# Loads of a feed-forward stage put in another order in a float32 decoder trunk on one TensorE

## The chip, the cores and the metric

The kernel runs on one core of a Trainium2 chip. The metric is the device time of one execution in microseconds (us); the kernel before takes 902.14 us, the median of three runs (898.80, 902.14 and 902.43). A profiled execution of its own took 899.16 us.

## The reference

The input x is 256 tokens by 1024 channels in float32. Two layers follow, each of three residual sub-layers: half a SwiGLU feed-forward, a token mixer, and half a second feed-forward. All weights are read once from HBM.

```python
for i in range(2):
    x = x + 0.5 * swiglu_ffn(rms_norm(x, ffn1_norm[i]), ffn1_w_in[i], ffn1_w_out[i])
    xn = rms_norm(x, mix_norm[i])
    y = pool_conv_mixer(xn, ...) if i % 2 == 0 else sgu_mixer(xn, ...)
    x = x + y
    x = x + 0.5 * swiglu_ffn(rms_norm(x, ffn2_norm[i]), ffn2_w_in[i], ffn2_w_out[i])
return rms_norm(x, final_norm)

def swiglu_ffn(x, w_in, w_out):              # w_in 1024 x 5632, w_out 2816 x 1024
    gate, up = jnp.split(x @ w_in, 2, axis=-1)
    return (jax.nn.silu(gate) * up) @ w_out
```

## The kernel before, in words

**Stages.** There are six, numbered k = 0 to 5: feed-forward (FFN), pooling and convolution mixer, FFN, FFN, gating mixer, FFN. So the four FFNs are stages 0, 2, 3 and 5; below they are the first to the fourth FFN.

**Slabs.** Weights arrive in slabs of 1 MB (128 partitions by 2048 floats, two DMAs of 512 KB each, issued by SP). Each slab is split into a high part (ScalarE, line 726, `w_hi`) and a low part (VectorE, line 1138, `w_lo`), since TensorE multiplies float32 as three products (lines 1676 to 1678). A slab of an FFN is named by its number in the stage, 0 to 38: slab 12 is `b + 12` in the code. Most slabs land in a ring of three raw buffers: a load waits until the low part of the slab three raw slabs earlier is done (line 349 is their DMA). Split slabs stand in a ring of six places.

**Units and pairs.** An FFN has eleven units of 256 hidden channels. Units 4 and 5, and again 8 and 9, are computed as a pair with seven block products instead of eight (the "seven", `SEVEN = (6, 21)`: the first pair begins at slab 6, the second at slab 21). The pair's four weight blocks lie in `quads[0..3]` (line 383; three in `scratch`, the fourth in `gain`, the tile that also holds the scales of the norms, so its load waits for the stage's norm, `xs_ready`). Sums of blocks are made in two ways: by VectorE (`weight_sum`, line 1395), and by two accumulating DMAs which GpSimd issues (`add_blocks`, lines 651 and 653). The first of them waits until quad 3 has landed, the second until slab 10 is split.

**Turns.** What a unit has computed is brought to the other layout through a transpose on VectorE (line 1330) and four SBUF-to-SBUF DMAs of 64 KB on SP's queue (`to_turn`, line 390); ScalarE then makes `act_hi` (line 853, `hidden_hi`) and VectorE `act_lo` (line 1337, `hidden_lo`). Turn d serves unit d-1, so the third turn serves the output step of unit 2. In VectorE's order the third `hidden_lo` stands ahead of the fourth unit's transposes, and these ahead of the side sums of tokens (line 1352) and of all that the pair needs.

**Output slabs.** Steps 0 to 3 of the output product use slabs 11, 12, 13 and 17; TensorE runs steps 0, 1 and 2 one after the other in the middle of the first pair (`outs(0)` to `outs(2)`), and step 3 near its end. The second pair does the same with slabs 26, 27, 28 and 32. The last three output slabs are 36, 37 and 38.

**Order.** Nothing plans the order: each engine's program is written out by hand, and so is SP's, which issues every weight load, every turn and the norm's scales (`gain_load`, line 402) in one sequence. Whatever SP waits for holds back all that is behind it. From slab 2 on, SP's sequence for the first pair is: units 1 and 2, quad 0, turn 1, slab 7, quad 2, slab 8, turn 2, quad 1, quad 3, slab 11, turn 3, slabs 12 and 13, turn 4, slab 17. `gain_load(k + 1)` is the last load of every stage.

Of the kernel before, what the change touches and what calls it, by code (L numbers as in the profile page):

```python
# [27 lines left out]
def hybrid_trunk(nc, x, ffn1_norm, ffn1_w_in, ffn1_w_out, mix_norm, ffn2_norm, ffn2_w_in, ffn2_w_out,  # L28
# [85 lines left out]
    with ExitStack() as ctx:  # L114
# [226 lines left out]
        def _(sp):  # L341
# [107 lines left out]
            for k, (kind, w_in, w_out, _) in enumerate(stages):  # L449
                b, d = base[k], ffn0[k]  # L450
                if kind == "ffn":
                    if k == 0:
                        load_x(0, 0)
                        load_quarters(0, w_in, 0, pair(0, FF))
                        load_x(1, 0)
                        load_x(0, 1)
                        load_x(1, 1)
                        load_quarters(1, w_in, 1, pair(0, FF))
                        load_rows(b + 2, w_in, 0, pair(WIDTH, FF))
                    elif stages[k - 1][0] != "ffn":  # L460
                        first_loads(k)
                    load_rows(b + 3, w_in, 1, pair(WIDTH, FF))

                    def out_of(v, n):

                        load_out(b + n, w_out, slice(2 * UNITS[v], 2 * UNITS[v] + 2))

                    z, y = SEVEN
                    load_unit(b + 4, w_in, 2)
                    if k:  # L470

                        sp.wait_ge(slab_used, b)
                        sp.wait_ge(xs_ready, 4 * k)
                    load_quad(0, w_in, 0, 4)
                    to_turn(d + 1)
                    load_rows(b + z + 1, w_in, 0, pair(3 * WIDTH, FF))
                    load_quad(2, w_in, 0, 5)
                    load_rows(b + z + 2, w_in, 1, pair(3 * WIDTH, FF))
                    to_turn(d + 2)
                    load_quad(1, w_in, 1, 4)  # L480
                    load_quad(3, w_in, 1, 5)
                    out_of(0, z + 5)
                    to_turn(d + 3)
                    out_of(1, z + 6)
                    out_of(2, z + 7)
                    to_turn(d + 4)
                    out_of(3, z + 11)
                    load_rows(b + 19, w_in, 0, pair(6 * WIDTH, FF))
                    load_rows(b + 20, w_in, 1, pair(6 * WIDTH, FF))
                    load_rows(b + y + 1, w_in, 0, pair(7 * WIDTH, FF))  # L490

                    sp.wait_ge(lo_split, b + z + T4 + 1)
                    load_quad(0, w_in, 0, 8)
                    load_quad(2, w_in, 0, 9)
                    to_turn(d + 5)
                    load_rows(b + y + 2, w_in, 1, pair(7 * WIDTH, FF))
                    load_quad(1, w_in, 1, 8)
                    to_turn(d + 6)
                    load_quad(3, w_in, 1, 9)
                    out_of(4, y + 5)  # L500
                    out_of(5, y + 6)
                    to_turn(d + 7)
                    out_of(6, y + 7)
                    to_turn(d + 8)
                    out_of(7, y + 11)
                    load_rows(b + 34, w_in, 0, pair((STEPS - 1) * WIDTH, FF))
                    load_rows(b + 35, w_in, 1, pair((STEPS - 1) * WIDTH, FF))
                    out_of(8, 36)
                    out_of(9, 37)
                    to_turn(d + 9)  # L510
                    out_of(10, 38)
                    to_turn(d + 10)
                    if k + 1 < len(stages):
                        first_loads(k + 1, d + STEPS)
                    else:
                        to_turn(d + STEPS)
                    if k == 0:

                        sp.wait_ge(lo_split, b + SUMS_END)
                        sp.dma_start(pw, pool_w[0].rearrange("g c d -> c g d")).then_inc(mix0_landed, 16)  # L520
                        sp.dma_start(tap_rows, conv_w[0]).then_inc(mix0_landed, 16)
                        rows = [pool_b[0], pool_scale[0].rearrange("(c p) -> c p", p=P),
                                conv_b[0].rearrange("(c p) -> c p", p=P),
                                conv_ln_g[0].rearrange("(c p) -> c p", p=P),
                                conv_ln_b[0].rearrange("(c p) -> c p", p=P)]
                        for r, src in enumerate(rows):
                            sp.dma_start(col_rows[r * CT:(r + 1) * CT, :], src).then_inc(mix0_landed, 16)
                    if k == 3:

                        sp.wait_ge(lo_split, b + SUMS_END)  # L530
                        sp.dma_start(ln_g, sgu_ln_g[0].rearrange("(a d) -> a d", a=1).broadcast_to([P, D]))\
                            .then_inc(mix1_landed, 16)
                        sp.dma_start(ln_b, sgu_ln_b[0].rearrange("(a d) -> a d", a=1).broadcast_to([P, D]))\
                            .then_inc(mix1_landed, 16)
                        sp.dma_start(scratch[:, 4096:4096 + HEADS * P],
                                     sgu_b[0].rearrange("(a h) s -> a (h s)", a=1).broadcast_to([P, HEADS * P]))\
                            .then_inc(mix1_landed, 16)
                elif kind == "mix0":
                    load_in(b + 3, ab_w_in[0], a_in + WIDTH)
                    for j in range(2):  # L540
                        load_rows(b + 4 + j, ab_w_in[0], j, pair(0, WIDTH))
                    for j in range(4):
                        load_out(b + 6 + j, ab_w_out[0], slice(2 * j, 2 * j + 2))
                else:
                    load_rows(b + 3, sgu_w_in[0], 1, pair(D + WIDE, WIDTH))
                    load_in(b + 4, sgu_w_in[0], 0)

                    sp.wait_ge(slab_used, b)
                    sp.dma_start(spatial_w, sgu_w[0].rearrange("h s t -> s h t"))\
                        .then_inc(spatial_landed, 16)  # L550
                    for j in range(1, 4):
                        load_in(b + 4 + j, sgu_w_in[0], j * WIDTH)
                    for j in range(4):
                        load_out(b + 8 + j, sgu_w_out[0], slice(2 * j, 2 * j + 2))
                gain_load(k + 1)


            for t in range(TT):
# [145 lines left out]
        def _(act):  # L704
# [197 lines left out]
            def seven(k, z, v):  # L902

                n, p, f = base[k] + z, len(SEVEN) * (ffn0[k] // STEPS) + SEVEN.index(z), fill0[k]
                split(n + 6)
                if z == SEVEN[0]:
                    side_hi_of(k, 2, 0)
                    side_hi_of(k, 3, 1)
                keep_first(k, z)
                split(n + 7)  # L910
                keep_in_gates(k, z, v, 1, T1, row[0])
                hidden_hi(k, v - 1)
                split(n + 8)
                split(n + 9)
                split(n + 10)
                split(n + 11)
                keep_in_gates(k, z, v, 0, T2, bank_x)
                split(n + 12)
                split(n + 13)
                gate_joined(0, p, k == 0)  # L920
                gate_joined(1, p, k == 0)
                gate_other(0, None, f + v + 1, side[0], k == 0)
                split(n + 14)
                hidden_hi(k, v)
                gate_other(1, n + T4 + 1, f + v + 1, bank_x, k == 0)

            for k, (kind, *_) in enumerate(stages):
# [9 lines left out]
                if kind == "ffn":  # L937
# [29 lines left out]
                    split(b + 10)  # L967
                    split(b + 11)
                    gates(3, 3, 7)
                    hidden_hi(k, 2)  # L970
                    seven(k, SEVEN[0], 4)
                    split(b + 21)
# [8 lines left out]
                    gate_of(0, 5, 7, 22)  # L981
                    split(b + 26)
                    gate_of(1, 5, 7, 22)
                    hidden_hi(k, 6)
                    seven(k, SEVEN[1], 8)
                    split(b + 36)
# [142 lines left out]
        def _(dve):  # L1129
# [272 lines left out]
            def seven(k, z, v):  # L1402
# [2 lines left out]
                late = k == 0  # L1405
                if z == SEVEN[0]:
                    side_sums(False)
                split(n + 6)
                if z == SEVEN[0]:
                    side_lo(k, 2, 0)  # L1410
                    side_lo(k, 3, 1)
                dve.wait_ge(kept, 3 * p + 1)
                join(p, n + B21 + 1, side[0], bank_z)
                split(n + 7)
                hidden_lo(k, v - 1)
                split(n + 8)
                split(n + 9)
# [31 lines left out]
            for k, (kind, *_) in enumerate(stages):  # L1449
# [11 lines left out]
                if kind == "ffn":  # L1461
# [36 lines left out]
                    half(3, 0)  # L1498
                    split(b + 11)
                    half(3, 1)  # L1500
                    blocks_of(3)
                    seven(k, SEVEN[0], 4)
                    split(b + 21)
# [8 lines left out]
                    half(7, 0)  # L1512
                    split(b + 26)
                    half(7, 1)
                    blocks_of(7)
                    seven(k, SEVEN[1], 8)
                    split(b + 36)
# [583 lines left out]
```

## Time and profile before

| | |
|---|---|
| median of three runs | 902.14 us (898.80 to 902.43) |
| profiled execution | 899.16 us |
| its span, first to last instruction | 897.4 us |
| TensorE busy | 868.6 us, 97% |
| VectorE busy | 699.1 us, 78% |
| ScalarE busy | 499.3 us, 56% |
| GpSimd busy | 92.4 us, 10% |
| moved by DMA | 198.71 MB, mean 221 GB/s |
| mean granted TensorE clock | 0.986 of full |

Matmuls are pipelined: of two that follow each other at the full clock each is shown as 0.39 us long, and they start 0.23 us apart. A row of waits says who waited for whom, with the total in us, how often, and the longest; a row of a timeline has the start, the length, engine, line and operation, and in brackets the idle time before it with what ended it.

### The profile page before, as it was taken

The page shows a single profiled execution, that of the slowest core. Times are in us where ns is not written, and L with a number is a line of the kernel's source. Part 1 is how long each engine was busy: PE and PEld are TensorE (multiplying, and loading weights), DVE is VectorE, ACT ScalarE, POOL GpSimd, SP SyncE. Part 2 cuts the span into 40 slices and gives each one's busy share as a digit, 9 for nine tenths or more (in the row PEclk, how much of TensorE's full clock was granted, in tenths as well). Part 3 has the DMA queues.
Part 4 walks back from the last instruction along what each step waited for, and adds up shares of the span by engine and source line. Part 5 has one row for each costly group of instructions (what it writes and reads, how often), then busy time and mean ns, then how long its engine had stood idle before and what let it go on. Part 6 is the DMA issues. An engine that isn't in the chain of part 4 may idle for free.

```text
span 897.4 us, 10578 instructions
## 1 busy us (share of the span) xinstructions
PE 868.6 (97%) x4006; PEld 721.7 (80%) x4006; DVE 699.1 (78%) x718; ACT 499.3 (56%) x543; POOL 92.4 (10%) x86
## 2 busy tenths in 40 slices
PE   9998999999999989999999899999799999899997
PEld 8786888878788868888888688888699888688886
DVE  5978887869967969687779597877597678778784
ACT  7547465557845745664537365735464445646543
POOL 0000000058820000000010000000200000000000
PEclk9999999999999999999999999999999999899999
DMA  8995995774255985984859959938584569679642
GB/s 281 313 264 173 285 280 184 223 227 168 91 187 160 287 258 189 298 263 153 272 155 286 269 161 319 272 134 264 186 315 148 160 189 263 229 223 294 200 150 83
DMA packets 155131, 198.71 MB, mean 221 GB/s; under 512 B 8461, under 2 KB 137513, under 8 KB 153032
## 3 DMA queue, kind: packets, MB, share of 16 engines
q1 hardware_dynamic: 152184, 180.72, 61.6%
q0 software_dynamic: 2304, 16.78, 9.3%
q8 instruction: 32, 0.52, 0.2%
q10 hardware_dynamic: 592, 0.53, 0.2%
q14 instruction: 19, 0.16, 0.0%
HBM read 168.11 MB, written 1.05 MB: 188 GB/s over the span
## 4 chain that ended last, share of the span: by engine, by line
PE 75%; DMA 8%; DVE 7%; ACT 4%; POOL 3%; SPq 1%; issue 1%; POOLq 0%; ACTq 0%; DVEq 0%
PE acc L1676 9%; PE acc L1677 9%; PE acc L1678 9%; PE ga L1676 7%; PE ga L1678 7%; PE ga L1677 7%; DMA raw<-in_ffn_w_out_dram 6%; PE ub L1678 5%; PE ub L1676 5%; PE ub L1677 5%; DVE w_lo L1138 4%; PE tp L1678 4%; PE tp L1676 4%; PE tp L1677 4%; ACT w_hi L726 3%; POOL w_lo L626 2%
## 5 line engine op out<-in xcount | busy, mean ns | idle before, releaser
L1138 DVE TENSOR_TENSOR w_lo<-raw,w_hi 128x2048 fp32r<-128x2048 f32 x111 | 253.6, 2292 | 45.2 <-ACT w_hi L726 44.9
L726 ACT ACTIVATE w_hi<-raw 128x2048 fp32r<-128x2048 f32 x119 | 226.4, 1909 | 40.5 <-DMA raw<-in_ffn_w_out_dram 35.2
L1676 PE MATMUL acc<-w_hi,act_hi 128*128 128x512 f32 x416 | 167.1, 402 | 14.4 <-DVE w_lo L1138 12.7
L1677 PE MATMUL acc<-w_lo,act_hi 128*128 128x512 f32 x416 | 164.7, 396 | 0.0
L1678 PE MATMUL acc<-w_hi,act_lo 128*128 128x512 f32 x416 | 164.5, 396 | 0.0
L1138 DVE TENSOR_TENSOR w_lo<-scratch,w_hi 128x2048 fp32r<-128x2048 f32 x48 | 109.0, 2285 | 4.6 <-ACT w_hi L726 4.5
L1676 PEld LDWEIGHTS acc<-w_hi,act_hi 128*128 128x128 f32 x416 | 80.3, 193 | 33.3 <-DVE w_lo L1138 14.4
L1676 PE MATMUL ga<-w_hi,xn_hi 128*128 128x512 f32 x256 | 101.1, 395 | 0.7 <-DVE sgh L1319 0.7
L1676 PE MATMUL ub<-w_hi,xn_hi 128*128 128x512 f32 x256 | 100.0, 390 | 0.3 <-DVE scratch L1309 0.3
L1678 PE MATMUL ga<-w_hi,xn_lo 128*128 128x512 f32 x256 | 99.8, 390 | 0.0
L1677 PE MATMUL ga<-w_lo,xn_hi 128*128 128x512 f32 x256 | 99.7, 390 | 0.0
L1677 PE MATMUL ub<-w_lo,xn_hi 128*128 128x512 f32 x256 | 99.7, 390 | 0.0
L1678 PE MATMUL ub<-w_hi,xn_lo 128*128 128x512 f32 x256 | 99.7, 389 | 0.0
L1678 PEld LDWEIGHTS acc<-w_hi,act_lo 128*128 128x128 f32 x416 | 80.0, 192 | 17.1
L1677 PEld LDWEIGHTS acc<-w_lo,act_hi 128*128 128x128 f32 x416 | 80.2, 193 | 16.0
L726 ACT ACTIVATE w_hi<-scratch 128x2048 fp32r<-128x2048 f32 x48 | 90.7, 1907 | 0.0
L853 ACT ACTIVATE act_hi<-xs 128x512 fp32r<-128x512 f32 x44 | 27.7, 630 | 77.4 <-DMA xs<-xs 77.3
L1337 DVE TENSOR_TENSOR act_lo<-xs,act_hi 128x512 fp32r<-128x512 f32 x44 | 30.3, 690 | 36.5 <-ACT act_hi L853 36.4
L1676 PEld LDWEIGHTS ga<-w_hi,xn_hi 128*128 128x128 f32 x256 | 48.1, 188 | 11.5 <-issue 1.5
L1676 PEld LDWEIGHTS ub<-w_hi,xn_hi 128*128 128x128 f32 x256 | 48.0, 188 | 11.1 <-DVE scratch L1309 0.7
L1678 PEld LDWEIGHTS ga<-w_hi,xn_lo 128*128 128x128 f32 x256 | 48.1, 188 | 10.2
L1678 PEld LDWEIGHTS ub<-w_hi,xn_lo 128*128 128x128 f32 x256 | 48.0, 188 | 10.1
(224 smaller groups left out, 1310.9 us busy)
## 6 DMA issues: line engine op xcount, KB each, us to landing
raw<-in_ffn_w_in_dram SPq DMA_DIRECT2D x108, 512.0 KB, 5.1
raw<-in_ffn_w_out_dram SPq DMA_DIRECT2D x88, 512.0 KB, 6.1
scratch<-in_ffn_w_in_dram SPq DMA_DIRECT2D x48, 512.0 KB, 6.2
scratch<-gain POOLq DMA_DIRECT2D x16, 1024.0 KB, 9.7
xs<-xs SPq DMA_DIRECT2D x176, 64.0 KB, 2.8
gain<-in_ffn_w_in_dram SPq DMA_DIRECT2D x16, 512.0 KB, 6.0
raw<-in_sgu_w_in_dram SPq DMA_DIRECT2D x16, 512.0 KB, 5.7
raw<-in_ab_w_in_dram SPq DMA_DIRECT2D x12, 512.0 KB, 5.7
```

The source lines that it names most:

```text
L626: pool.tensor_tensor(w_lo[:, slot_of[n], :], slab(n), w_hi[:, slot_of[n], :].bitcast(F32), ALU.subtract).then_inc(lo_split, 1)
L726: act.activation(w_hi[:, slot_of[n], :], slab(n), ACT.Copy).then_inc(hi_split, 1)
L853: act.activation(by_quarters(act_hi, v % 4), turn, ACT.Copy).then_inc(h_hi_done, 1)
L1138: dve.tensor_tensor(w_lo[:, slot_of[n], :], slab(n), w_hi[:, slot_of[n], :].bitcast(F32), ALU.subtract).then_inc(lo_split, 1)
L1337: dve.tensor_tensor(by_quarters(act_lo, v % 4), turn, by_quarters(act_hi, v % 4).bitcast(F32), ALU.subtract).then_inc(h_done, 1)
L1676: pe.matmul(dst, s_hi, m_hi, start=start, stop=False, skip_group_check=onto)
L1677: pe.matmul(dst, s_hi, m_lo, start=False, stop=False, skip_group_check=onto)
L1678: return pe.matmul(dst, s_lo, m_hi, start=False, stop=stop, skip_group_check=onto)
```

## The change

In an FFN that is not the first stage, SP loads quad 0 ahead of slab 3 (behind a wait for the mixer's last use of `scratch`) and quad 2 ahead of slab 4, both before `xs_ready`, which is waited for only ahead of slab 11. Quad 1 goes ahead of slab 8. In every FFN slab 11 goes ahead of quad 3, and slabs 12 and 13 go ahead of the third turn; nothing stands between the third and the fourth turn. The scales of the next stage's norm are loaded behind slab 37 instead of at the stage's end. ScalarE and VectorE split slab 12 (and 27) ahead of the third (seventh) hidden part, and slab 13 (28) where slab 12 (27) was split.

```diff
+                    if k and stages[k - 1][0] == "mix0":
+                        sp.wait_ge(mix_ready, 4)
+                    elif k and stages[k - 1][0] == "mix1":
+                        sp.wait_ge(gu_done, 4)
+                    if k:
+                        load_quad(0, w_in, 0, 4)
                     load_rows(b + 3, w_in, 1, pair(WIDTH, FF))
...
+                    if k:
+                        load_quad(2, w_in, 0, 5)
                     load_unit(b + 4, w_in, 2)
-                    if k:
-
-                        sp.wait_ge(slab_used, b)
-                        sp.wait_ge(xs_ready, 4 * k)
-                    load_quad(0, w_in, 0, 4)
+                    if k == 0:
+                        load_quad(0, w_in, 0, 4)
                     to_turn(d + 1)
                     load_rows(b + z + 1, w_in, 0, pair(3 * WIDTH, FF))
-                    load_quad(2, w_in, 0, 5)
+                    if k == 0:
+                        load_quad(2, w_in, 0, 5)
+                    else:
+                        load_quad(1, w_in, 1, 4)
                     load_rows(b + z + 2, w_in, 1, pair(3 * WIDTH, FF))
                     to_turn(d + 2)
-                    load_quad(1, w_in, 1, 4)
+                    if k == 0:
+                        load_quad(1, w_in, 1, 4)
+                    else:
+                        sp.wait_ge(xs_ready, 4 * k)
+                    out_of(0, z + 5)
                     load_quad(3, w_in, 1, 5)
-                    out_of(0, z + 5)
-                    to_turn(d + 3)
                     out_of(1, z + 6)
                     out_of(2, z + 7)
+                    to_turn(d + 3)
                     to_turn(d + 4)
                     out_of(3, z + 11)
...
                     out_of(8, 36)
                     out_of(9, 37)
+                    sp.wait_ge(lo_split, b + SUMS_END)
+                    gain_load(k + 1)
                     to_turn(d + 9)
                     out_of(10, 38)
...
# ScalarE's seven(); VectorE's is changed in the same places
-                split(n + 6)
+                split(n + 7)
                 if z == SEVEN[0]:
                     side_hi_of(k, 2, 0)
                     side_hi_of(k, 3, 1)
                 keep_first(k, z)
-                split(n + 7)
...
# ScalarE's FFN stage; likewise split(b + 27) ahead of hidden_hi(k, 6)
                     gates(3, 3, 7)
+                    split(b + 12)
                     hidden_hi(k, 2)
                     seven(k, SEVEN[0], 4)
```

## Rows read from the trace of the kernel before

**Rows 1.** The page: TensorE's busy time, and DMA busy tenths in 40 slices.
```profile
PE 868.6 (97%) x4006; PEld 721.7 (80%) x4006; DVE 699.1 (78%) x718; ACT 499.3 (56%) x543; POOL 92.4 (10%) x86
DMA  8995995774255985984859959938584569679642
```

**Rows 2.** Waits of TensorE: waiter, releaser, total us, times, longest.
```profile
PE acc L1676 <- DVE w_lo L1138: 12.7, 4, 3.7
PE tp L1750 <- DVE xs L1188: 5.9, 2, 5.3
```

**Rows 3.** Windows: stretch, length, each engine's busy us, PE clock, DMA share, GB/s.
```profile
65.00:80.00 15.00, 11.93 (x47) 9.45 (x46) 9.37 (x9) 10.50 (x10) 0.00 (x0) 0.89 0.78 265
505.00:520.00 15.00, 11.34 (x44) 8.95 (x44) 8.97 (x7) 10.17 (x10) 0.00 (x0) 0.89 0.73 249
765.00:780.00 15.00, 12.03 (x41) 9.36 (x40) 9.66 (x9) 10.51 (x10) 0.00 (x0) 0.77 0.76 263
...
780.00:795.00 15.00, 15.00 (x68) 12.43 (x67) 12.96 (x8) 7.98 (x7) 0.00 (x0) 1.00 0.36 115
...
622.00:642.00 20.00, 14.72 (x63) 11.87 (x61) 10.91 (x13) 6.38 (x12) 5.60 (x3) 0.91 0.79 263
441.00:461.00 20.00, 20.00 (x97) 16.34 (x96) 14.04 (x18) 9.07 (x15) 5.95 (x3) 1.00 0.77 254
```

**Rows 4.** The chain of waits: start, length, what.
```profile
494.13 13.16 DMA raw<-in_ffn_w_out_dram
...
621.04 9.96 DMA gain<-in_mix_norm_dram
```

**Rows 5.** Timeline of SP in the third FFN, first pair.
```profile
480.20 1.06 SPq L383 DMA_DIRECT2D gain<-in_ffn_w_in_dram  x2
...
488.85 3.66 SPq L390 DMA_DIRECT2D xs<-xs  x4
492.55 7.35 SPq L349 DMA_DIRECT2D raw<-in_ffn_w_out_dram  x4
```

**Rows 6.** Timeline of SP in the third FFN, second pair.
```profile
548.99 2.12 SPq L349 DMA_DIRECT2D raw<-in_ffn_w_out_dram  x4
559.63 2.74 SPq L390 DMA_DIRECT2D xs<-xs  x4
```

**Rows 7.** Timeline of GpSimd in the third FFN: the adding DMAs.
```profile
488.84 0.89 POOL L651 DMA_DIRECT2D scratch<-gain  x1 [36.02 <-DMA gain<-in_ffn_w_in_dram]
493.64 0.86 POOL L653 DMA_DIRECT2D scratch<-gain  x1 [3.91 <-DVE w_lo L1138]
554.11 0.86 POOL L651 DMA_DIRECT2D scratch<-gain  x1 [59.61 <-DMA gain<-in_ffn_w_in_dram]
```

**Rows 8.** Windows of 2 us in the third FFN.
```profile
492.00:494.00 2.00, 2.00 (x11) 1.65 (x10) 1.34 (x1) 0.75 (x1) 0.36 (x1) 1.00 0.99 196
...
556.00:558.00 2.00, 2.00 (x11) 1.65 (x10) 2.00 (x2) 2.00 (x2) 0.00 (x0) 1.00 1.12 373
...
560.00:562.00 2.00, 2.00 (x10) 1.68 (x9) 2.00 (x2) 0.00 (x0) 0.00 (x0) 1.00 1.02 213
```

**Rows 9.** Timeline of ScalarE in the third FFN: third and seventh hidden part.
```profile
498.71 0.63 ACT L853 ACTIVATE act_hi<-xs 128x512 fp32r<-128x512 f32 x1 [1.23 <-DMA xs<-xs]
...
565.73 0.63 ACT L853 ACTIVATE act_hi<-xs 128x512 fp32r<-128x512 f32 x1 [0.38 <-DMA xs<-xs]
```

**Rows 10.** Timeline of VectorE: low parts of slabs 12 and 13, third FFN.
```profile
509.25 2.29 DVE L1138 TENSOR_TENSOR w_lo<-raw,w_hi 128x2048 fp32r<-128x2048 f32 x1 [4.65 <-ACT w_hi L726]
...
515.21 2.29 DVE L1138 TENSOR_TENSOR w_lo<-raw,w_hi 128x2048 fp32r<-128x2048 f32 x1 [1.11 <-ACT w_hi L726]
```

**Rows 11.** Timelines of VectorE (join, slab 23) and TensorE (slab 23), second FFN.
```profile
348.25 0.69 DVE L1400 TENSOR_TENSOR sgh<-ga,sgh 128x512 f32<-128x512 f32 x1 [0.77 <-PE ga L1678]
...
375.45 2.29 DVE L1138 TENSOR_TENSOR w_lo<-raw,w_hi 128x2048 fp32r<-128x2048 f32 x1 [1.31 <-ACT w_hi L726]
...
377.89 0.41 PE L1676 MATMUL ga<-w_hi,xn_hi 128*128 128x512 f32 x1
```

More of the change, by code:

```diff
@@ L517, in _ @@
                     if k == 0:
-                        sp.wait_ge(lo_split, b + SUMS_END)
                         sp.dma_start(pw, pool_w[0].rearrange("g c d -> c g d")).then_inc(mix0_landed, 16)
@@ L528, in _ @@
                     if k == 3:
-                        sp.wait_ge(lo_split, b + SUMS_END)
                         sp.dma_start(ln_g, sgu_ln_g[0].rearrange("(a d) -> a d", a=1).broadcast_to([P, D]))\
@@ L543, in _ @@
                         load_out(b + 6 + j, ab_w_out[0], slice(2 * j, 2 * j + 2))
+                    gain_load(k + 1)
                 else:
@@ L554, in _ @@
                         load_out(b + 8 + j, sgu_w_out[0], slice(2 * j, 2 * j + 2))
-                gain_load(k + 1)
+                    gain_load(k + 1)
             for t in range(TT):
@@ L983, in _ @@
                     gate_of(1, 5, 7, 22)
+                    split(b + 27)
                     hidden_hi(k, 6)
@@ L1407, in seven @@
                     side_sums(False)
-                split(n + 6)
+                split(n + 7)
                 if z == SEVEN[0]:
@@ L1413, in seven @@
                 join(p, n + B21 + 1, side[0], bank_z)
-                split(n + 7)
                 hidden_lo(k, v - 1)
@@ L1500, in _ @@
                     half(3, 1)
+                    split(b + 12)
                     blocks_of(3)
@@ L1514, in _ @@
                     half(7, 1)
+                    split(b + 27)
                     blocks_of(7)
```

## The prediction

> **What bounds the kernel now.** I read the page first, then the waits of TensorE, the windows around them, the chain of waits, and last the timelines of SP, GpSimd, ScalarE and VectorE in one FFN. The page says TensorE is busy 97% of the span [rows 1], so only what fills its gaps, or shortens its work, can help. Its waits show two large kinds [rows 2]: four waits of the output product for a low part, 12.7 us together, and two transposes that waited 5.9 us for the normed tokens. The reader should see "4 times" and think "once in each FFN".
>
> The windows price them, because they hold the slow clock behind a stall as well [rows 3]. At full pace 15 us start 68 matmuls. Around the stall of the first FFN there are 47, so (68 - 47) x 15/68 = 4.6 us are lost; the second FFN shows the same count. The third has 44: 5.3 us. The fourth has 41: 6.0 us. The 20 us around the norm of the gating mixer hold 63 matmuls and transposes, where the same work two stages earlier holds 97: 20 x 34/97 = 7.0 us. The granted clock in these windows is 0.77 to 0.91 of full, that is partly the 1.2 GHz level, and 1.00 in the clean ones. Together 4.6 + 4.6 + 5.3 + 6.0 = 20.5 us for the FFNs and 7.0 us for the norm: 27.5 us.
>
> What ends the FFN stall is a load: slab 12, on its way 13.16 us, from 494.13 to 507.29 [rows 4]. It was issued behind the third turn (488.85) at 492.55 [rows 5], when the first adding DMA of GpSimd (488.84) was already running and the second (493.64) about to be issued [rows 7]. While an add runs, the DMA engines are full at only 196 to 213 GB/s; plain loads of output slabs run at 373 [rows 8]. The norm of the gating mixer waited for a load of 0.5 MB of scales, 9.96 us long, issued at 621.04 as SP's last load of the stage, behind three others [rows 4].
>
> **The change, part by part.**
>
> *Slabs 12 and 13 ahead of the third turn.* Slab 12 needs the buffer of slab 7, slab 13 that of slab 8; both are free by the time the third turn can be issued, since VectorE splits them ahead of the transposes that the turn waits for. So slab 12 is issued right behind quad 3 (480.20 in the third FFN [rows 5]), about where slab 11 was, and slab 13 just before 488.85. With nothing but plain loads ahead, slab 12, in slab 11's old place in the queue, lands before the first add starts: well over 10 us earlier than 507.29. Its stall goes whole: 20.5 us over four FFNs.
>
> The price is the third turn, now behind slab 13, and the adds. What an add does to such a queue can be read in the second pair, where slabs 26 and 27 are already issued ahead of turn and add: they are issued at 548.99 [rows 6], the add at 554.11 [rows 7], yet 556 to 558 still moves 373 GB/s and only 560 to 562 shows the add's 213 [rows 8]. So the add stood back until the loads issued before it were through. The seventh turn, issued at 559.63 during the add, reached ScalarE at 565.73 [rows 6, 9], after the add was through. In order of issue, then: the new third turn comes one slab later than before. 1.05 MB at 373 GB/s is 2.8 us, with the issue of two more DMAs some 3.3 us: 498.71 [rows 9] becomes about 502.
>
> Who waits for it: VectorE's third hidden part stands ahead of the fourth unit's transposes, the side sums and the low parts of the pair. Before, VectorE had done all of this and stood idle for 4.65 us ahead of slab 12's low part, and 1.11 us ahead of slab 13's [rows 10]. The third turn may be 4.65 us later before VectorE is later than it was. Since slab 12's low part moves into earlier idle time and slab 13's takes its place, the 1.11 us and the 2.2 us of one low part go too; ScalarE's conversions that must then follow take back some 1.5. I put the break-even at 6.4 us. 3.3 is less, so VectorE comes out about 3 us ahead of its old course.
>
> That must suffice farther on. The join in front of slab 18 waited 0.77 us for TensorE [rows 11], and slab 23's low part ended at 375.45 + 2.29 = 377.74, only 0.15 us before TensorE took it at 377.89. Between the two lies a string: slab 18, then the second pair's quads, the fifth turn, VectorE's sum, ScalarE's negation, slab 23. So TensorE keeps a lead only as far as VectorE's join comes earlier too: 3.1 us from above, 0.77 from the join's own wait, 0.15 of margin, some 4.0 of 4.6 to 6.0. In the first FFN slab 11 is also ahead of quad 3, so the add starts one slab later, but there the third turn is issued before the add. I take 0.8 us per FFN as given back, 3 us in all; bounds are 0 and 8.
>
> *Quads 0 and 2 early.* Four DMAs in each of three FFNs move ahead of slabs 3 and 4, into a time when DMA is idle: the 31st to 33rd slices before the fourth FFN's pair show 4, 5 and 6 tenths, the 34th, over the pair, 9 [rows 1]. The trace doesn't show a slab 3 behind a quad. At best, less traffic in the pair lets the later loads land up to the same 5.6 us (2.1 MB at 373) earlier, which frees nothing once the stall is gone; at worst slab 3 is 2.8 us late in three stages, 8 us. The added waits (`mix_ready`, `gu_done`) hold SP, and behind it slabs 3 to 5, until the mixer's last hidden part, about when slab 3's buffer comes free anyway. I take 0; the idle slices hide it.
>
> *The scales ahead of the last output slab.* 0.5 MB at 373 GB/s is 1.4 us, plus one issue, moved ahead of two turns and slab 38 in every FFN. The same load goes from the stage's end. At worst 1.8 us in each of four, 7 us; at best only the norm's gain. I take 0 for the price, because the load passes in front of the ninth turn, two output steps before the stage's last. `lo_split` is met by then (slab 36's own load waits longer). The gain is the norm's 7.0 us: the load starts some 20 us earlier and its 9.96 us end before the tokens are ready. Next late there is GpSimd's root and VectorE's scaling, as in every other norm.
>
> *Slab 27 and 28 split ahead of the seventh hidden part.* 2.3 us of VectorE move ahead of the eighth turn, which then stands behind the second add anyway. I take 0; bounds -1 and +2.
>
> Sum: 20.5 + 7.0 - 3 = 24.5 us off 899.16 (the span of 897.4 and 1.8 around it) gives 874.7. The median shown is 3 us above the profiled execution, which is near the lowest; a median after should stand between, so I say 876 us.
>
> A rule of the Trainium skill speaks against this order. "DMA: Bandwidth & Descriptors", section "Queues, rings and completion order", says that each engine goes round-robin between the queue rows that have work, packet by packet. By it the add would start in the midst of slab 13 and the small packets of the turn would take turns with the second add's large ones, landing only with it; the sum would then be the rival at 892 below. The second pair's windows, 373 GB/s until the loads were through, don't agree with it for the start of an add.
>
> **The rivals.**
> 1. VectorE becomes the bound: half of the FFN gain comes back as waits at slab 23 and in the pair's second half. 20.5/2 + 7 = 17: about 883. For it: the margin of 0.15 us; against it, the 4.65 us of idle time.
> 2. The third turn misses the space between the two adds and lands with the second, about 507 instead of 498.71, 8.3 us later. That is 1.9 beyond the break-even; the stall moves to slab 13 and the first added block, and the FFNs gain nothing: 899.2 - 7 = 892. For it: an add keeps turns out altogether (559.63 to 565.73). Against it: the order of issue.
> 3. Slower. The same late turn, but VectorE can make up only its idle 4.65 us: 8.3 - 4.65 = 3.7 us late at the join, of which slab 23's margin takes 0.15 in the second FFN. Four times 3.5 is 14 us over the old course, less 7: 906. It decides when the third turn lands more than 4.65 us later than before.
>
> The change does what it says in any case: the loads are in SP's program order.
>
> **How the numbers follow.** The forecast, 870 to 880, has a chance of 0.60, rival 1 0.20, rival 2 0.12, rival 3 0.08. No stall left anywhere and no give-back is 871.7 by the profiled time. The range from 868 to 894 holds the first two and most of rival 2. Half a percent, 4.5 us, is what a measurement can tell from no change. Faster: 0.60 + 0.20 + 0.05, the part of rival 2 that stays clear of that bound, = 0.85; same 0.08, the rest of rival 2 and the mildest of rival 3; slower 0.07.
>
> **What would show it.** Right: the waits of TensorE have neither the four at L1138 nor the two at L1188; 15 us windows in the pairs hold 68 matmuls; the third hidden part in the third FFN starts some 3 us later relative to its stage. Wrong: waits of TensorE for low parts at slab 13, 14 or 23, a third hidden part behind the second add, or a wait at slab 3 or 4 of a later FFN.

## The result and the profile after

The changed kernel takes 888.59 us (median of 4 runs, 886.76 to 890.44), the kernel before beside it 900.47: a ratio of 0.987, 95% interval 0.983 to 0.991. The forecast was 876. The direction and the range held; of the 24.5 us forecast, the medians show 11.9 and the profiled executions 8.9 (spans 897.4 and 888.5). The account below is of the profiled executions.

In kernel.py of the changed kernel the slab matmuls are L1691 to L1693 (before: L1676 to L1678), low parts L1152 (L1138), `act_hi` L866 (L853), `act_lo` L1351 (L1337), the norm's scaling L1202 (L1188), the adding DMAs L664 and L666 (L651, L653).

The page's two lines of [rows 1]: TensorE has lost 3.7 us of busy time, and still shows 97%.
```profile
PE 864.9 (97%) x4006; PEld 716.4 (81%) x4006; DVE 696.8 (78%) x718; ACT 499.1 (56%) x543; POOL 92.9 (10%) x86
...
DMA  8995995755167965995859759957685659579651
```
The waits of TensorE, against [rows 2]. The four at slab 12 are gone, and of the two at a norm the one of 5.3 us; the other, 0.7 us at the first mixer's norm, is still there. In their place each of the last three FFNs waits for low parts in the pair (slabs 14 and 17, in the second FFN also 13) and for gate and product ahead of slab 22, and each of the first three waits for `act_lo` of its last turn ahead of slab 38 (in the first FFN it did so before, 1.0 us of it).
```profile
PE acc L1691 <- DVE act_lo L1351: 5.4, 3, 2.8
PE ga L1691 <- DVE sgh L1337: 3.4, 3, 1.4
PE tp L1691 <- DVE w_lo L1152: 2.7, 3, 1.3
PE acc L1691 <- DVE w_lo L1152: 1.7, 4, 0.9
```
Windows, against [rows 3] (stretch, length, busy us of each engine, clock, DMA share, GB/s). The first FFN's stall holds 68 matmuls where it held 47, the third FFN's 68 where it held 44. But the window behind it holds 62, and that over slabs 21 to 23 holds 58.
```profile
65.00:80.00 15.00, 15.00 (x68) 12.39 (x67) 12.76 (x12) 10.08 (x9) 0.00 (x0) 1.00 0.74 235
501.00:516.00 15.00, 15.00 (x68) 12.43 (x67) 11.09 (x14) 8.25 (x9) 0.00 (x0) 1.00 0.61 198
...
517.00:532.00 15.00, 14.39 (x62) 11.62 (x63) 14.97 (x11) 8.35 (x8) 0.00 (x0) 1.00 0.36 108
...
545.00:560.00 15.00, 13.41 (x58) 10.45 (x57) 11.71 (x10) 10.01 (x9) 0.86 (x1) 1.00 0.96 290
```
To say where time comes and goes I took TensorE's first matmul of each slab in both traces; the lead is how much earlier it starts than before. Columns two to four are changes of the lead, in us; the sums are of unrounded values:

| | stall at slabs 12, 13 removed | given back by slab 24 | lost at the stage's end | third turn, issue to last landing (before) |
|---|---|---|---|---|
| FFN 1 | 4.7 | 0.0 | 1.0 | 10.7 (9.9) |
| FFN 2 | 4.8 | 5.1 | 1.1 | 17.1 (9.1) |
| FFN 3 | 5.3 | 3.8 | 4.6 | 15.3 (9.8) |
| FFN 4 | 6.1 | 3.2 | 0.0 | 15.1 (10.2) |
| norm of the gating mixer | 7.0 | | | |

21.0 + 7.0 - 12.1 - 6.7 = 9.2, less 0.2 that the profiled execution started later: 9.0, and the lead at the last slab is 8.95.

The give-back starts with the third turn. The chain of waits in the third FFN (start, length, what):
```profile
488.04 1.93 SPq L390
...
490.01 11.94 DMA xs<-xs
...
501.97 0.64 ACT act_hi L866
```
Timelines of SP, then GpSimd (SPq is SP issuing a DMA; x4 are four of them): slab 13 goes out at 484.86, the first add at 485.58, the four parts of the turn from 486.61 (the fourth at 490.01), and the second add 1.4 us after that.
```profile
484.86 0.80 SPq L349 DMA_DIRECT2D raw<-in_ffn_w_out_dram  x2
486.61 4.97 SPq L390 DMA_DIRECT2D xs<-xs  x4
```
```profile
485.58 0.89 POOL L664 DMA_DIRECT2D scratch<-gain  x1 [35.00 <-DMA gain<-in_ffn_w_in_dram]
491.41 0.86 POOL L666 DMA_DIRECT2D scratch<-gain  x1 [4.93 <-DVE w_lo L1152]
```
A turn signals its landing 64 times, 16 for each part. 48 had come by 496.34, with the first add (496.21). The last came at 501.94, the second add at 501.76.

The packets show how. The adds are on queue q0, the slabs' loads and the turns on q1 (queue, packets, MB, busy share of 16 engines). From 491.5 to 494.0 the first add's packets of 8 KB and the turn's of 512 B go one for one. The last 30 of the turn's 512 packets go only after 500.9, when the second add's are through (below the dots, 500.9 to 502.0; six of the 36 are of 4 bytes).
```profile
q0 software_dynamic: 61, 0.50, 99.8%
q1 hardware_dynamic: 61, 0.03, 6.3%
...
q1 hardware_dynamic: 36, 0.02, 5.2%
```

VectorE, against [rows 10]: it idles 3.27 us for the turn, and its low part of slab 14 starts at 514.90 and ends at 517.19; TensorE, which waits for it, starts slab 14 at 517.34.
```profile
502.63 0.69 DVE L1351 TENSOR_TENSOR act_lo<-xs,act_hi 128x512 fp32r<-128x512 f32 x1 [3.27 <-ACT act_hi L866]
...
514.90 2.29 DVE L1152 TENSOR_TENSOR w_lo<-scratch,w_hi 128x2048 fp32r<-128x2048 f32 x1 [1.11 <-ACT w_hi L739]
```

### The profile page after: what moved, and what is told of

It is laid out like the page before. It is cut to its first block, busy times and chain, and to the rows that moved or that the text cites. A ratio compares the mean times of both kernels' runs of the same rounds, so it can differ in the third digit from the quotient of the medians.

```text
span 888.5 us, 10579 instructions
## 1 busy us (share of the span) xinstructions
PE 864.9 (97%) x4006; PEld 716.4 (81%) x4006; DVE 696.8 (78%) x718; ACT 499.1 (56%) x543; POOL 92.9 (10%) x86
## 4 chain that ended last, share of the span: by engine, by line
PE 51%; DVE 23%; DMA 9%; ACT 5%; issue 5%; SPq 3%; POOL 3%; POOLq 0%; ACTq 0%; DVEq 0%
DVE w_lo L1152 11%; DMA xs<-xs 9%; PE acc L1691 6%; PE acc L1692 6%; PE acc L1693 6%; PE ga L1691 5%; PE ga L1693 5%; PE ga L1692 5%; PE ub L1692 3%; PE ub L1693 3%; PE ub L1691 3%; SPq L390 3%; DVE xs L1344 3%; ACT w_hi L739 3%; POOL w_lo L639 2%
## 5 line engine op out<-in xcount | busy, mean ns | idle before, releaser
L1152 DVE TENSOR_TENSOR w_lo<-raw,w_hi 128x2048 fp32r<-128x2048 f32 x111 | 253.6, 2291 | 30.7 <-ACT w_hi L739 30.1
L1691 PE MATMUL acc<-w_hi,act_hi 128*128 128x512 f32 x416 | 164.3, 395 | 7.8 <-DVE act_lo L1351 5.4
L1692 PE MATMUL acc<-w_lo,act_hi 128*128 128x512 f32 x416 | 162.4, 390 | 0.0
L1693 PE MATMUL acc<-w_hi,act_lo 128*128 128x512 f32 x416 | 162.4, 390 | 0.0
L1152 DVE TENSOR_TENSOR w_lo<-scratch,w_hi 128x2048 fp32r<-128x2048 f32 x48 | 109.0, 2284 | 9.0 <-ACT w_hi L739 8.9
L1691 PE MATMUL ga<-w_hi,xn_hi 128*128 128x512 f32 x256 | 101.5, 397 | 4.4 <-DVE sgh L1337 3.4
L1691 PEld LDWEIGHTS acc<-w_hi,act_hi 128*128 128x128 f32 x416 | 78.5, 189 | 27.1 <-issue 8.0
L1691 PE MATMUL ub<-w_hi,xn_hi 128*128 128x512 f32 x256 | 99.8, 390 | 0.3 <-DVE scratch L1323 0.3
L1693 PE MATMUL ga<-w_hi,xn_lo 128*128 128x512 f32 x256 | 99.8, 390 | 0.0
L1693 PE MATMUL ub<-w_hi,xn_lo 128*128 128x512 f32 x256 | 99.7, 389 | 0.0
L1693 PEld LDWEIGHTS acc<-w_hi,act_lo 128*128 128x128 f32 x416 | 78.5, 189 | 16.5
L1692 PEld LDWEIGHTS acc<-w_lo,act_hi 128*128 128x128 f32 x416 | 78.5, 189 | 15.6
L866 ACT ACTIVATE act_hi<-xs 128x512 fp32r<-128x512 f32 x44 | 27.7, 629 | 103.6 <-DMA xs<-xs 103.6
L1351 DVE TENSOR_TENSOR act_lo<-xs,act_hi 128x512 fp32r<-128x512 f32 x44 | 30.3, 690 | 55.1 <-ACT act_hi L866 55.1
L1691 PEld LDWEIGHTS ga<-w_hi,xn_hi 128*128 128x128 f32 x256 | 48.1, 188 | 17.0 <-issue 5.4
L1691 PEld LDWEIGHTS ub<-w_hi,xn_hi 128*128 128x128 f32 x256 | 48.0, 188 | 11.0 <-DVE scratch L1323 0.7
L1693 PEld LDWEIGHTS ga<-w_hi,xn_lo 128*128 128x128 f32 x256 | 48.1, 188 | 10.1
L1693 PEld LDWEIGHTS ub<-w_hi,xn_lo 128*128 128x128 f32 x256 | 48.1, 188 | 9.9
```

The lines of the kernel that those rows point to most:

```text
L866: act.activation(by_quarters(act_hi, v % 4), turn, ACT.Copy).then_inc(h_hi_done, 1)
L1152: dve.tensor_tensor(w_lo[:, slot_of[n], :], slab(n), w_hi[:, slot_of[n], :].bitcast(F32), ALU.subtract).then_inc(lo_split, 1)
L1351: dve.tensor_tensor(by_quarters(act_lo, v % 4), turn, by_quarters(act_hi, v % 4).bitcast(F32), ALU.subtract).then_inc(h_done, 1)
L1691: pe.matmul(dst, s_hi, m_hi, start=start, stop=False, skip_group_check=onto)
L1692: pe.matmul(dst, s_hi, m_lo, start=False, stop=False, skip_group_check=onto)
L1693: return pe.matmul(dst, s_lo, m_hi, start=False, stop=stop, skip_group_check=onto)
```

## The experiments

Ratios are to the kernel before on the same chip; its median was 897.6, 897.4, 904.4 and 901.8 us on the four chips (experiments 1 to 4, 5 to 8, 9 to 12, 13 and 14). Its runs fall into two groups, around 897 and around 904 us, in another mix on each chip, and no run shows why. So between chips a ratio can be off by some half a percent: experiment 9's kernel ran 872.2 and 872.1 us on two chips, at 0.964 and 0.967. The changed kernel is 0.987 (888.59 us).

**1. The scales' move alone**, on the kernel before.
```diff
                     out_of(9, 37)
+                    sp.wait_ge(lo_split, b + SUMS_END)
+                    gain_load(k + 1)
                     to_turn(d + 9)
...                  # the load at the stage's end goes, in an FFN
```


> The kernel before, with nothing changed but the scales' load, which goes ahead of the ninth turn instead of the stage's end. Theory A (the scales' place is worth the whole wait of the norm, and costs only where TensorE has run ahead of VectorE at a stage's end): the four waits for slab 12 stay, the two at the norm's scaling (5.9 us) go, some 7 us less than the kernel before, about 893. The ninth turn lands some 1.5 us later than before relative to its issue. Theory B (the load in front of the ninth turn delays the stage's last output steps by its own 1.4 to 1.8 us in each of four FFNs): only 0 to 2 us less, about 899.


0.997 (0.994 to 1.000), some 2.7 us. The norm gains 6.9 us of lead, but the ends of FFNs 1, 2 and 3 lose 2.6, 1.0 and 1.1. Theory B has its price about right (4.7 us in all), theory A the norm. The waits (five at low parts, since slab 13 of the fourth FFN now waits too):
```profile
PE acc L1679 <- DVE w_lo L1141: 13.5, 5, 3.9
PE acc L1679 <- DVE act_lo L1340: 3.8, 3, 2.0
```

**2. The changed kernel with the scales' load back at the stage's end.**

> The changed kernel with the scales' load back at the end of each stage. Theory A (the late third turn is what took back 3 to 4 us in each pair; the scales' place matters for the norm, and for the end of the third FFN): the norm of the gating mixer waits some 7 us again, the end of the third FFN loses some 2 us less than the 4.6 us that it loses in the changed kernel: 888.6 + 7 - 2, about 893 to 894. Theory B (the scales' place costs nothing at the stage's end): about 895.6, the ninth turn landing no sooner after its issue than the 5.8 us of the changed kernel.


0.994 (0.991 to 0.997). The ends lose nothing, so the price is the scales' own. But the norm of the first mixer, which did not wait before, now loses 6.2 us as well: with TensorE 5 us ahead there the old place is too late for it too. Before its price, the move is worth 7 us alone and 13 behind a faster FFN. Neither theory had this.
```profile
PE tp L1766 <- DVE xs L1203: 9.3, 3, 5.2
```

**3. The third turn ahead of slab 13 again.**
```diff
                     out_of(1, z + 6)
-                    out_of(2, z + 7)
                     to_turn(d + 3)
+                    out_of(2, z + 7)
```


> The changed kernel with the third turn issued ahead of slab 13 again (slab 12 stays ahead of it), in all four FFNs. Theory A (the fourth part of the third turn is caught behind the second add, and this is what VectorE is late by): all four parts land by about 496.5 in the third FFN instead of 501.94, the waits ahead of slabs 14 to 23 fall from 3.2 to 4.0 us to under 1 in each of the last three FFNs, and some 8 us go, about 880; slab 13 lands with the second add's neighbours, at worst near 505, still ahead of its turn on VectorE. Theory B (the pair is slow after slab 12 because more loads and adds than before share it, wherever the turn stands): same as the changed kernel, within 2 us. Theory C (slab 13 takes over slab 12's old stall): slower than the changed kernel by 5 to 10 us.


0.979 (0.975 to 0.983); 879.96 us. The third turn takes 6.1, 8.9, 9.6 and 7.5 us in the four FFNs, 12.1 us given back become 3.8 (3.3 of them ahead of slabs 22 and 23 of FFNs 2 and 4), and slab 13 costs nothing. Theory A, though the second FFN still gives back 2.0 and the fourth 1.3, more than its 1.

**4. The second add behind the turn**, SP's order as in the changed kernel.
```diff
                 pool.wait_ge(lo_split, n + T1 + 1)
+                pool.wait_ge(turn_landed, 64 * turns)
                 pool.dma_start(quads[0], quads[3], accum_op=ALU.add)...
```


> The changed kernel; GpSimd issues the second adding DMA of each pair only when the third (seventh) turn has landed. The order of SP is the changed kernel's. Theory A: the third turn is whole by about 497 in the third FFN instead of 501.94; the second add starts some 2 us later and lands near 504 instead of 501.76, ahead of its users; the waits ahead of slabs 14 to 23 fall to under 1 us per FFN, some 8 us go, about 880. Theory B (VectorE is late for the pair's loads as such): same as the changed kernel within 2 us, with VectorE's third hidden part early all the same. Theory D (the second add is itself what slabs 17 to 23 wait for): slower than the changed kernel by about 2 us in each of eight pairs, with waits at the sum of the second add's quads.


0.977 (0.973 to 0.981); 876.65 us. Theory A again, though the turn was not as early as it said in the first FFN (13.5 us; 10.4 to 10.9 in the others). GpSimd and ScalarE in the third FFN:
```profile
482.18 0.89 POOL L664 DMA_DIRECT2D scratch<-gain  x1 [35.14 <-DMA gain<-in_ffn_w_in_dram]
494.42 0.86 POOL L667 DMA_DIRECT2D scratch<-gain  x1 [11.35 <-DMA xs<-xs]
```
```profile
493.91 0.63 ACT L868 ACTIVATE act_hi<-xs 128x512 fp32r<-128x512 f32 x1 [0.46 <-DMA xs<-xs]
```
The turn starts 10.9 us after its issue instead of 15.4, and the pair of the third FFN gives nothing back; the second add, 11.4 us behind the turn's issue instead of 4.8, stalls nobody there. The first FFN still gives back 1.9 us.

**5. Quads 0 and 2 back in the pair**, and with them quad 1 behind slab 8 (the slabs' and scales' moves kept). In the first FFN, which has no early quads, nothing was given back; I suspected them.

> The changed kernel with the first pair's quads 0 and 2 loaded in the pair again, in the last three FFNs, as in the kernel before and as in the first FFN of the changed one; slabs 12 and 13 stay ahead of the third turn and the scales ahead of slab 38. Theory A (the early quads bring the first add ahead of the third turn, so that the turn's last part falls behind the second add; the first FFN, without them, gave nothing back): the third turn is issued before the first add or has landed before the second in all four FFNs, the 11 us given back in the pairs fall to some 2, about 880. Theory B (the two more slabs ahead of the turn are what make it late, the quads only lighten the pair): the third turn lands with the second add or later still, about 2 us more in each of three FFNs, about 892 to 895.


0.989 (0.984 to 0.994). Theory A is wrong: the third turn takes 17.5, 18.6 and 14.3 us in FFNs 2 to 4. In the third it starts still later:
```profile
508.37 0.63 ACT L852 ACTIVATE act_hi<-xs 128x512 fp32r<-128x512 f32 x1 [8.14 <-DMA xs<-xs]
```

**6. The scales one place later.**
```diff
-                    sp.wait_ge(lo_split, b + SUMS_END)
-                    gain_load(k + 1)
                     to_turn(d + 9)
+                    sp.wait_ge(lo_split, b + SUMS_END)
+                    gain_load(k + 1)
                     out_of(10, 38)
```


> The changed kernel with the scales' load one place later: behind the ninth turn, still ahead of slab 38. Theory A (in front of the ninth turn the load costs it its own 1.4 to 1.8 us, and the last output steps hang on that turn): the ninth turn of the third FFN lands 4 us after its issue, not 5.8; the losses at the stage ends (1.0, 1.0 and 4.6 us) fall by 1.0, 1.0 and 1.7; the norm's 7 us stay; about 885. Theory B (the last steps hang on the eleventh turn, behind the next stage's first loads): the ninth turn is earlier, the eleventh lands at the same time, no change of more than 1 us.


0.983 (0.977 to 0.989), runs from 877.6 to 890.7. Theory A: the ninth turn takes 4.0 us, not 5.8, no stage's end loses, and the norm still gains 6.9. In the profiled execution the first FFN's third turn took 18.8 us, with the adds issued much as in the changed kernel, and gave back 6.8 us: 60 of its 64 signals were there by 56.66, the last came at 67.59 with the second add. So which side of the add a turn falls on seems a matter of luck in each FFN. I take that for the 13 us between this kernel's runs, as its other runs have no trace.

**7. The last turn between the next stage's first two slabs.**
```diff
                 for j in range(2):
+                    if j and turned is not None:
+                        to_turn(turned)
                     ...load_rows(base[k] + j, ...)
-                if turned is not None:
-                    to_turn(turned)
```


> The changed kernel with a stage's last turn issued between the first and the second slab of the next stage, not behind both; the scales stay in front of the ninth turn. Theory A (the scales in front of the ninth turn set the stage's end): the eleventh turn lands some 3 us earlier, but the wait ahead of it moves to the tenth: 1 to 2 us less than the changed kernel, about 887. Theory B (the eleventh turn waits in the queue behind 2 MB of the next stage's slabs): the wait of 2.9 us for it in the third FFN goes, and that of 1 us in the first and second, some 4 us less, about 884.5. Theory C (the next stage's second slab comes late for it): the gain is lost again at the next stage's start.


0.997 (0.993 to 1.001), about 9 us worse than the changed kernel: theory C. In front of the third FFN the second slab, issued at 436.36, lands at 441.62, and VectorE splits it ahead of the norm it owes. TensorE loses 6.0 us there, 5 of the gating mixer's 7 are not gained.
```profile
436.36 5.26 DMA raw<-in_ffn_w_in_dram
...
441.64 1.93 ACT w_hi L739
...
443.59 2.29 DVE w_lo L1152
```

**8. The orders of 4, 6 and 7 together.**

> The changed kernel with three orders of loads changed together: the second add behind the third (seventh) turn, the scales behind the ninth turn, the last turn between the next stage's first two slabs. If the three losses are apart from each other: the ratio of second_add_behind_turn_3, 0.9765 of the kernel before, less 3 to 5 us that its stage ends still lost: about 873. If the stage ends hang on something else (VectorE's work as such): the same as second_add_behind_turn_3, 876.6.


0.984 (0.979 to 0.988), worse than 4 alone. No loss of over 0.5 us is left in a pair or at an end except at the norms (8.6 us of waits), which are the price of 7. Neither number was right.

**9. The orders of 4 and 6.**

> The changed kernel with two of the three orders: the second add behind the third (seventh) turn, the scales behind the ninth turn; the last turn stays behind both first slabs of the next stage. Theory A (what the kernel with three orders lost, it lost at the norms, since the slab that the norm's engines convert first came late behind the last turn): no wait of over 1 us at a norm but the gating mixer's 7 us still gained, no loss of 1 to 1.5 us at the ends of the first and third FFN: some 3 us less than the kernel with the second add alone (0.9765 of the kernel before), about 873. Theory B (the three orders spoil each other in another way): 880 or more.


**0.964** (0.962 to 0.967); 872.21 us. Theory A. The lead over the kernel before is 25.8 us at the last slab. The page and the largest waits left:
```profile
PE 860.3 (99%) x4006; PEld 716.1 (82%) x4006; DVE 697.1 (80%) x718; ACT 498.9 (57%) x543; POOL 92.7 (11%) x86
```
```profile
PE ga L1918 <- POOL avg L583: 1.2, 1, 1.2
PE acc L1693 <- DVE act_lo L1353: 1.0, 1, 1.0
```

**10. The orders of 3, 4 and 6.**

> As the kernel with the second add behind the turn and the scales behind the ninth turn, with the third turn ahead of slab 13 as well. Theory A (a late turn is the whole give-back of the pair): the third turn lands 6 to 9 us after its issue in all four FFNs instead of 10 to 13, the 1.7 us at slabs 22 and 23 of the first FFN go, about 871 to 872. Theory B (with the second add held, VectorE has slack in every pair): the same time as without it, within 1 us.


0.964 (0.961 to 0.966); 871.91 us. The turn takes 5.8 to 9.5 us, as theory A said, and it changes nothing, as theory B said.

**11. The kernel before with experiment 4's wait and nothing else.**

> The kernel before with one wait more: GpSimd issues the second adding DMA of a pair when the third (seventh) turn has landed. No load moves, the scales stay at the stage's end. Theory A (slab 12's stall was the second add in front of it in the DMA engines, not its place in SP's order): the third turn lands near 498.7 in the third FFN as before, slab 12, issued at 492.55, lands at 501 to 502 instead of 507.29, the four waits at slab 12 (20.5 us) go or nearly; the norm's 7 us stay, about 878 to 880. Theory B (slab 12 needs its place ahead of the turn): slab 12 lands with the first add or behind the second all the same, at most 5 us less than the kernel before; or a late second add stalls slabs 17 to 23.


0.978 (0.975 to 0.981); 884.73 us. One wait is worth more than the whole change. Slab 12, still behind the turn, is issued at 486.94, lands between the first add (493.99) and the second (504.23), and is converted at 496.84:
```profile
483.43 3.46 SPq L390 DMA_DIRECT2D xs<-xs  x4
486.94 5.14 SPq L349 DMA_DIRECT2D raw<-in_ffn_w_out_dram  x4
```
```profile
483.47 0.89 POOL L651 DMA_DIRECT2D scratch<-gain  x1 [36.06 <-DMA gain<-in_ffn_w_in_dram]
495.14 0.86 POOL L654 DMA_DIRECT2D scratch<-gain  x1 [10.78 <-DMA xs<-xs]
```
```profile
494.63 0.63 ACT L855 ACTIVATE act_hi<-xs 128x512 fp32r<-128x512 f32 x1 [2.57 <-DMA xs<-xs]
496.84 1.92 ACT L728 ACTIVATE w_hi<-raw 128x2048 fp32r<-128x2048 f32 x1 [1.58 <-DMA raw<-in_ffn_w_out_dram]
```
Some 20 of the FFNs' 21.0 us are gained: theory A. As in 2, the first mixer's norm then loses 4.9 us, which theory A did not have: the profiled execution is 15.6 us shorter (spans 897.4 and 881.8), not 20. That the ratio still gives theory A's number (0.978 of 899.2 is 879) is in part luck, since all nine runs of the kernel before on this chip took 902.4 us or more.

**12. Experiment 9 with quads 0 and 2 back in the pair.**

> As the kernel with the second add behind the turn and the scales behind the ninth turn, with quads 0 and 2 of the last three FFNs loaded in the pair again. Theory A (the quads' early place is worth nothing once nothing stalls in the pair): the same time within 1 us. Theory B (2 MB less in the pair is what keeps the turn and the adds early enough): 1 to 3 us more in each of three FFNs, with waits at slabs 14 to 23.


0.966 (0.964 to 0.969); 874.16 us. 2 us worse than 9 by the medians and by the profiled leads (23.8 against 25.8): theory B in kind, of a third of the size.

**13. and 14. The orders of 4 and 6 on the kernel before, beside experiment 9 again.** Slabs and quads stay where they were.

> The kernel before with the second add behind the third (seventh) turn and the scales behind the ninth turn; slabs 12 and 13 and quads 0 and 2 stay where they were. Theory A (with the second add held, slab 12 is through between the adds, and its place ahead of the turn is worth only the last stall that is left): the norms' 7 and 5 us go as well, and what remains against the kernel with the change's order is 0.5 to 2 us, waits at slabs 12 and 13 of the third FFN; ratio to the kernel before some 0.966. Theory B (the slabs' order carries a part of its own, more than 4 us): 0.970 or more.

> The changed kernel with the second add behind the turn and the scales behind the ninth turn, run again beside no_slab_order: 0.9641 of the kernel before, within its interval.


0.968 (0.964 to 0.972), 873.02 us, and 0.967 (0.964 to 0.971), 872.13 us. Once the second add is held and the scales are in place, the change's order of slabs and quads is worth 0.9 us, which these runs don't tell from nothing.

## Why the prediction was wrong

**The stalls: right.** Forecast 20.5 us in the FFNs and 7.0 at the norm, removed 21.0 and 7.0.

**The third turn: the step that failed.** "In order of issue, then: the new third turn comes one slab later than before", 3.3 us, 498.71 to about 502. In the time of the trace it came to just that, 501.97, by luck: the third FFN had 2.2 us of lead by then, and in its own frame the turn was 5.5 us late, in FFN 2 8.0 and in FFN 4 4.9. The order of issue holds, in the main, for slab 13 against the first add, whose first packet came at 489.01, 3.4 us after its issue. It does not protect the turn: its packets went one for one with the add's, and its last signals came with the second add, issued 1.4 us after the fourth part. That is rival 2's mechanism, to which I gave 0.12. Experiment 4, which takes the second add away from the turn and moves nothing else, and 3, which takes slab 13 from in front of it, both remove most of the give-back (3.3 and 3.8 us are left of 12.1); 5 shows that the early quads are not its cause.

**The give-back: 12.1 us, not 3.** It follows from that step, and my break-even of 6.4 us passes the test. Behind the turn VectorE should be 6.4 less the lateness ahead of its old course: -1.6, 0.9 and 1.5 us in FFNs 2 to 4 (in the third, slab 14's low part is 3.1 us earlier, 2.2 of it lead). TensorE kept -0.2, 1.5 and 2.9 of the stalls, 0.6 to 1.4 more; I had named 0.9 for the join's wait and slab 23's margin. The 3 us were also too few by the prediction's own terms: 4.0 kept of 4.6, 4.6, 5.3 and 6.0 leaves 4.5 given back. Slab 23 has 0.05 us of margin in three or all four FFNs of every trace with the changed order of slabs, also in experiment 9's; with the slabs where they were, in experiment 13, it has 0.4 to 1.6.

**The scales: a price of 0 taken, 6.7 us measured.** I had written bounds of 0 to 7 and taken the end that favoured the change, because the load "passes in front of the ninth turn, two output steps before the stage's last". But the ninth turn is itself late for VectorE at full pace: in the third FFN it went from 4.0 to 5.8 us, VectorE idled 3.6 us for it, and the tenth and eleventh followed (4.1 to 4.9 and 4.6 to 6.8 us). Experiment 1 shows the price without the rest of the change, 6 and 9 that one place later is free.
```profile
595.11 0.37 SPq L402 DMA_DIRECT2D gain<-in_mix_norm_dram  x1
596.20 2.51 SPq L390 DMA_DIRECT2D xs<-xs  x4
```
```profile
602.03 0.63 ACT L866 ACTIVATE act_hi<-xs 128x512 fp32r<-128x512 f32 x1 [5.27 <-DMA xs<-xs]
...
619.54 0.63 ACT L866 ACTIVATE act_hi<-xs 128x512 fp32r<-128x512 f32 x1 [4.45 <-DMA xs<-xs]
```

**Early quads: 0 taken.** Alone 2 us (0.989 in experiment 5 against 0.987, within the intervals), 2 us in 12 (the intervals of 9 and 12 overlap there too). No wait at slab 3 or 4 came.

**Rivals.** 888.6 lies between rival 1 (883) and rival 2 (892). In terms: removed 28.0, given back 18.8 instead of 3. Of that excess 9.1 belong to the turn and 6.7 to the scales.

The rule that I set against the order of issue, of the Trainium skill ("DMA: Bandwidth & Descriptors", section "Queues, rings and completion order"), said that the turn would land only with the second add. For the turn the trace agrees in three FFNs of four, and so do the 61 packets of each queue between 491.5 and 494.0. The same section says that a DMA's completion signal lands only after every earlier write of the same engine, across its queues. The runs here don't test that: the turn's data were late themselves, the last packet starting at 501.44, the last signal coming at 501.94.

What stays open: why 1.0 to 2.9 us between the issue of a turn's last part and that of the second add are enough in one execution and not in another. One difference can be seen in the packets. Before, slab 12 was issued between the two, and the second add's first packet came 1.4 to 2.7 us after the first add's last; in the changed kernel nothing was, and it came within 0.4 us. Experiment 3, with slab 13 behind the turn, has 1.3 to 1.6 us again in FFNs 2 to 4. No run changes this alone, and the first FFN, whose turn is issued ahead of the first add, was late in experiment 6 and not in the changed kernel with the same gap.

## What to carry to other kernels

When a load is late behind a large DMA of another queue, ask first whether that DMA can be held until the small transfer has landed: here one wait, on an engine that is 10% busy, did more than the whole change of order. Work out each moved transfer's lateness relative to the lead that the change itself creates; every stage after the first gain runs against the same loads with less time. And where a bound reaches from 0 to the size of the gain, take a value inside it unless a row shows idle time at the very place.

## What the runs showed of the hardware

- A 64 KB part of a turn that is issued 1.0 to 2.9 us ahead of a 1 MB adding DMA can land with that DMA: such turns took 15.1 to 18.8 us where turns with free DMA engines took 4.0. In one case 60 of 64 signals came 11 us before the last.
- While both had work, the engines moved one 512 B packet of the turn for each 8 KB packet of the add (61 and 61 in 2.5 us), and an 8 KB packet took 0.63 us.
- An adding DMA's first packet came 1.4 us after its issue where no load was in flight (experiment 4, the second adds of the first pairs) and 2.6 to 3.5 us after it behind loads (the first adds of the changed kernel). That is no rule: in experiment 11 it came after 1.7 us with loads moving 425 GB/s. A turn issued before an add was not safe from it.
- 0.5 MB of scales, broadcast to 128 partitions, in front of the ninth turn cost it 1.5 to 1.8 us in FFNs 2 to 4 (4.0 to 5.8 in the third), about the 1.4 us that 373 GB/s give, or a little over.
